# Norm, routing and token lists behind an output projection: block norms on VectorE, one routing chain for four blocks, ranks summed on TensorE, lists from rounded products

## What is computed

```python
x = layer_norm(DN_ALPHA * x + m, ln1_g[i], ln1_b[i])     # m: mixer output times w_o
f = hier_moe(x, ...)
x = layer_norm(DN_ALPHA * x + f, ln2_g[i], ln2_b[i])

def hier_moe(x, w_rg, b_rg, w_re, b_re, w1, w3, w2):
    g_prob = softmax(xt @ w_rg + b_rg)                   # 4 groups
    grp = argmax(g_prob); g_w = g_prob[grp]
    e_logits = (xt @ w_re + b_re).reshape(N, 4, 8)[grp]  # the 8 experts of that group
    top_v, top_i = lax.top_k(e_logits, 2)
    gate = softmax(top_v) * g_w
    expert = grp * 8 + top_i
    # every expert gets the list of its tokens; for each list:
    hdn = silu(xb @ w1[e]) * (xb @ w3[e])
    out[tokens] += (hdn @ w2[e]) * w
```

## Time and profile before

| | us |
|---|---|
| median of 3 runs | 3568.32 |
| fastest, slowest | 3567.33, 3570.15 |
| the profiled execution, its time | 3554.19 |
| its span | 3552.9 |

### The profile page before, as it was taken

How to read it: one execution, slowest core, us unless ns; L and a number is a source line. 1 busy time by engine, 2 the same in 40 slices (tenths; PEclk the granted TensorE clock), 3 DMA queues, 4 the chain that set the end, 5 groups by cost and what they waited for, 6 DMA issues and landing times. The chain is left out here.

```text
span 3552.9 us, 42265 instructions
## 1 busy us (share of the span) xinstructions
PE 3270.6 (92%) x16668; PEld 2719.4 (77%) x16669; DVE 2241.1 (63%) x3508; ACT 1801.9 (51%) x2689; POOL 394.9 (11%) x331
## 2 busy tenths in 40 slices
PE   8989899999989999999987999999789879999995
PEld 6789777877878777878766777788667868888874
DVE  5755343435855443333675888899743668988886
ACT  3333342323333342333462778888633628888884
POOL 1101000000101000000141111111100121111110
PEclk9988999999989999999998999999989989999998
DMA  4210122221120122222203899988722238898994
GB/s 139 72 56 1 64 79 95 95 81 63 50 80 1 48 95 75 93 88 89 72 1 110 327 351 364 359 348 353 301 71 103 80 144 336 357 361 356 361 359 178
DMA packets 135163, 590.99 MB, mean 166 GB/s; under 512 B 29616, under 2 KB 35632, under 8 KB 110256
## 3 DMA queue, kind: packets, MB, share of 16 engines
q1 hardware_dynamic: 115664, 569.92, 41.5%
q0 software_dynamic: 19296, 18.30, 2.2%
HBM read 594.40 MB, written 44.04 MB: 180 GB/s over the span
## 5 line engine op out<-in xcount | busy, mean ns | idle before, releaser
L189 PE MATMUL ps<-r,r 128*128 128x512 f32 (+4 forms) x11048 | 2593.7, 393 | 66.8 <-DVE r L2075 23.1
L189 PEld LDWEIGHTS ps<-r,r 128*128 128x128 f32 x11048 | 2046.2, 190 | 536.8 <-issue 63.8
L3463 DVE TENSOR_TENSOR r<-mem,r 128x1024 fp32r<-128x1024 f32 x768 | 902.5, 1220 | 133.6 <-ACT r L3408 127.3
L3408 ACT ACTIVATE r<-mem 128x1024 fp32r<-128x1024 f32 x768 | 788.3, 1061 | 226.5 <-PE ps L189 144.4
L692 ACT ACTIVATE r<-mem 128x512 fp32r<-128x512 f32 (+3 forms) x518 | 338.7, 661 | 906.4 <-PE ps L189 900.0
L727 DVE TENSOR_TENSOR r<-mem,r 128x512 fp32r<-128x512 f32 (+1 forms) x272 | 185.5, 688 | 436.6 <-ACT r L692 435.5
L729 DVE SCALAR_TENSOR_TENSOR r<-mem,r 128x512 fp32r<-128x512 f32 (+3 forms) x246 | 171.7, 714 | 263.6 <-ACT r L692 261.9
L3321 POOL DMA_INDIRECT xa<-mem,memu x64 | 101.5, 1587 | 964.7 <-ACT mem L3433 964.7
L3261 POOL DMA_INDIRECT mem<-xd,memu x64 | 99.2, 1550 | 84.2 <-PE ps L3343 35.1
L1666 PE MATMUL ps<-mem 128*128 128x65 f32 x800 | 99.8, 282 | 0.0
L1666 PEld LDWEIGHTS ps<-mem 128*128 128x128 f32 x800 | 96.7, 199 | 0.0
(11 more groups left out here) (392 smaller groups left out, 2883.2 us busy)
## 6 DMA issues: line engine op xcount, KB each, us to landing
mem<-in_w_up SPq DMA_DIRECT2D x80, 2048.0 KB, 18.5
mem<-in_w_down SPq DMA_DIRECT2D x80, 2048.0 KB, 7.9
mem<-in_w_gate SPq DMA_DIRECT2D x64, 2048.0 KB, 13.2
mem<-in_w_in SPq DMA_DIRECT2D x10, 2048.0 KB, 7.9
mem<-in_odd_w_qkv SPq DMA_DIRECT2D x6, 2048.0 KB, 8.4
mem<-in_w_o SPq DMA_DIRECT2D x4, 2048.0 KB, 10.4
mem<-in_rel SPq DMA_DIRECT2D x16, 512.0 KB, 3.3
mem<-in_even_w_in SPq DMA_DIRECT2D x3, 2048.0 KB, 8.0
```

The source lines that it names most:

```text
L189: r = e.matmul(out, a, b, start=start and i == 0, stop=stop and i == n - 1, skip_group_check=skip)
L3408: act.e.activation(wh, w, ACT.Copy).then_inc(*self.S["ex_wh"](self.l, e, i))
L3463: dve.e.tensor_tensor(wl, w, wh.bitcast(F32), SUB).then_inc(*self.S["ex_wl"](self.l, e, i))
```

## The change

All blocks' norms are on VectorE now, block t's between block t's moments and block t+1's sum; ScalarE's and GpSimd's parts are gone. The logits of blocks 0 and 1 are corrected among the blocks. TensorE computes the logits three matmuls later, and the logits of block 2 ahead of the turning of block 3. The group is found by a maximum and an equality, with the first among equals kept by a minimum; the masks of four blocks are made and added in one instruction each. TensorE adds the totals of earlier blocks onto the ranks by three more products in the same PSUM bank, so VectorE reads finished ranks. The comparison that makes `OS` is two instructions of 512, with rounded output. `OV` is rounded too: GpSimd writes the token number less 1024 (exact), the rounded gate, and what the rounding left out, 96 columns instead of 64. An empty place gives 0, and 0 + 1024 is a row beyond the end.

```diff
 # pe_blocks
-                if i == n - 3:
-                    if j >= 1:
-                        self.pe_turn(pe, j - 1)
-                    if j >= 2:
-                        self.pe_logits(pe, j - 2)
+                if i == n - 3 and j >= 1:
+                    self.pe_turn(pe, j - 1)
+                if i == n - 2 and j >= 2:
+                    self.pe_logits(pe, j - 2)
+        self.pe_logits(pe, 2)
         self.pe_turn(pe, 3)
-        self.pe_logits(pe, 2)
         self.pe_logits(pe, 3)
 # pe
-        pe.e.matmul(K.bank[0][:, 0:128], self.ustr, self.ohs, start=True, stop=True)
-        pe.e.matmul(K.bank[0][:, 128:256], self.ones, self.ohs, start=True, stop=True).then_inc(*S["rt_p"](l, "rank"))
-        pe.wait_ge("rt_v", l, "os")
-        mm(pe.e, K.bank[1][:, 0:64], [(self.OS[:, k, t, :], self.OV[:, k, t, :]) for k in range(2) for t in range(4)]).then_inc(
-            *S["rt_p"](l, "lists"))
+        pe.e.matmul(bank[:, 0:128], self.ustr, ohs, start=True, stop=False, skip_group_check=True)
+        for t in range(3):
+            o = bank[:, 32 * t + 32:128].rearrange("p (t n) -> p t n", n=32)
+            r = pe.e.matmul(o, self.ones, bc(ohs[:, 32 * t:32 * t + 32], 1, 3 - t), start=False, stop=t == 2,
+                            skip_group_check=True)
+        r.then_inc(*S["rt_p"](l, "rank"))
...
+        pe.wait_ge("rt_g", l, "values")
+        for k in range(2):
+            pe.wait_ge("rt_v", l, "os", k)
+            for t in range(4):
+                r = pe.e.matmul(K.bank[1][:, 0:96], self.OS[:, k, t, :], self.OV[:, k, t, :], start=k == 0 and t == 0,
+                                stop=k == 1 and t == 3)
+        r.then_inc(*S["rt_p"](l, "lists"))
 # dve_blocks
+        def norm(t):
+            x = K.X[:, t, :]
+            dve.wait_ge("d_ln", self.gains.names)
+            dve.wait_ge("rt_p", self.l, "turn", t, 1)
+            dve.then("ln_g", v.scalar_tensor_tensor(x, x, self.nmu[:, t:t + 1], self.gains.gb, ADD, MUL), sid, t)
+            v.scalar_tensor_tensor(x, x, self.mv[:, t, 1:2], self.gains.bb, MUL, ADD).then_inc(*S["ln_b"](sid, t))
         for t in range(4):
+            if t:
+                norm(t - 1)
+            if t == 3:
+                self.logits(dve, 0)
...
             job.dves(dve, self, job, t, self.acc(job, t)[:, 0:job.n])
             moments(t)
...
             roots(t)
+        self.logits(dve, 1)
+        norm(3)
 # route
+        dve.then("rt_v", v.tensor_reduce(self.gm, groups, AX.X, MAX))
+        v.tensor_tensor(goh, groups, bc(self.gm, 2, 4), ALU.is_equal).then_inc(*S["rt_v"](l, "goh"))
+        v.tensor_tensor(ge, groups, bc(self.gm, 2, 4), SUB).then_inc(*S["rt_v"](l, "ge"))
+        dve.wait_ge("rt_v", l, "goh")
+        dve.then("rt_v", v.tensor_tensor(goh, goh, bc(self.first, 1, 4), MUL))
+        dve.then("rt_v", v.tensor_reduce(self.mn, goh, AX.X, MIN))
+        dve.then("rt_v", v.tensor_tensor(goh, goh, bc(self.mn, 2, 4), ALU.is_equal))
+        dve.then("rt_v", v.tensor_scalar(goh, goh, 1.0, 1e30, SUB, MUL))
+        dve.then("rt_v", v.tensor_tensor(ml.rearrange("p t (g n) -> p t g n", g=4),
+                                         lg[:, :, 4:36].rearrange("p t (g n) -> p t g n", g=4), bc(goh, 3, 8), ADD))
...
+        dve.then("rt_v", v.tensor_tensor(oh, bc(bc(ei, 1, 4), 1, 2), bc(which, 3, 32), ALU.is_equal), l, "oh")
 # lists
+        dve.wait_ge("rt_p", l, "rank")
+        ranks = bank[0][:, 0:128].rearrange("p (t n) -> p t n", t=4)
+        dve.then("rt_v", v.tensor_tensor(self.ranked, self.oh, bc(ranks, 1, 2), MUL))
+        dve.then("rt_v", v.tensor_reduce(self.rv.rearrange("p t k -> p k t"), self.ranked, AX.X, ADD))
+        for k in range(2):
+            v.tensor_tensor(self.OS[:, k], bc(self.iota, 1, 4), bc(self.rv[:, :, k], 2, 128),
+                            ALU.is_equal).then_inc(*S["rt_v"](l, "os", k))
...
+        dve.then("rt_v", v.tensor_scalar(self.ixf, bank[1][:, 0:32], NONE, None, ADD))
+        v.tensor_copy(self.IDX[:, 1, :], self.ixf).then_inc(*S["rt_v"](l, "rows"))
+        dve.then("rt_v", v.tensor_copy(self.GT, bank[1][:, 32:64]))
+        v.tensor_tensor(self.GT, self.GT, bank[1][:, 64:96], ADD).then_inc(*S["rt_v"](l, "weights"))
 # pool
-            pool.wait_ge("ln_a", sid, t)
-            pool.then("ln_g", pool.e.tensor_tensor(x, x, self.gains.gb, MUL), sid, t)
-            pool.then("ln_b", pool.e.tensor_tensor(x, x, self.gains.bb, ADD), sid, t)
+        pool.wait_ge("rt_v", l, "oh")
+        p.tensor_tensor(OV[:, :, :, 0:32], self.oh, bc(self.val.rearrange("p t k -> p k t"), 3, 32), MUL)
+        pool.wait_ge("rt_v", l, "gt")
+        pool.then("rt_g", p.tensor_tensor(self.gates, self.oh, bc(self.gt.rearrange("p t k -> p k t"), 3, 32), MUL))
+        pool.then("rt_g", p.tensor_copy(OV[:, :, :, 32:64], self.gates))
+        p.tensor_tensor(OV[:, :, :, 64:96], self.gates, OV[:, :, :, 32:64].bitcast(F32), SUB).then_inc(*S["rt_g"](l, "values"))
```

141 lines of the change are left out of this document (43 added, 98 removed).

## The result

| | before | changed |
|---|---|---|
| median of the first comparison, us | 3567.82 (4 runs) | 3538.23 (4 runs, 3535.69 to 3547.28) |
| all runs of this study | 3567.2 (52 runs, 3550.2 to 3578.7) | 3541.2 (16 runs, 3524.8 to 3553.7) |
| the profiled execution, its span | 3554.19, 3552.9 | 3547.28, 3546.0 |

The ratio of the first comparison is 0.9932, 95% interval 0.9914 to 0.995. Two repeats, on two chips, gave 0.991 (0.9891 to 0.993) and 0.9938 (0.9919 to 0.9957).

A forecast was written before the change was run, and what follows sets the result against it. A serial chain, nearly all on VectorE, from the last block's sum to the first expert gather was taken as the bound. Gains 4.4 + 2.7 + 1.1 + 1.6 + 0.45 = 10.3 per layer: 3568.3 - 20.5 = 3547.8 us, range 3541 to 3556.

The forecast's parts named there:

- stall ahead of block 1's transposes: TensorE, ready to turn block 1, waits for block 0's norm and block 1's sum on VectorE: some 0.75 us.
- Step A: Norm of all blocks on VectorE, up to the route's start: 4.4 us gained per layer, give or take 1.
- step C: Ranks, gates and list operands, from `ohs` to the first list product: 5.25 us instead of 6.38, 1.1 gained per layer.
- rival (1): TensorE drops to half clock among the blocks: 3575.7 us, chance 0.03 in full; only after block 3, costs 1 to 2.
- Step B: The route for all blocks, up to `ohs`: 3.55 us instead of 6.24, 2.7 gained per layer.
- Step D: TensorE's list products: eight rounded matmuls in 2.1 us instead of sixteen passes in 3.67, 1.6 gained per layer (0.2 to 2.0).
- Step E: From the lists to the first gather: two small steps go, 0.45 us gained per layer.
- The difference between the profiled execution and the median: The median was 14.1 us longer than the profiled execution before; the forecast took this difference as unchanged.
- (2): VectorE and GpSimd collide more, GpSimd's operations taking twice the rows' size: 2.7 us more per layer, 3553.1 us, chance 0.08.
- (3): L3177's long steps were no waits for GpSimd, small two-input steps stay at 2.2 in places: 3557.3 us, chance 0.04.
- (4): Expert weights hold the start up, so an earlier gather is followed by a longer wait: 3566.3 us, chance 0.05.

The follow-up runs named there:

- no_pool_norm: The kernel before with GpSimd's six norm operations left out (no gain and bias for blocks 1 to 3): 3559.07 us in one run.
- norm_undone: The changed kernel with the norm as before and the logit corrections of blocks 0 and 1 behind the blocks again: 3550.95 us, ratio 0.9969.
- after_third: The changed kernel itself, measured a third time beside the kernel before: 3546.05 us (6 runs), ratio 0.9938.
- values_dve: The changed kernel with GpSimd's four operations for the list operands moved to VectorE: 3543.46 us (7 runs), ratio 0.9932.
- after_again: The changed kernel itself, measured again on another chip beside the kernel before: 3535.85 us (6 runs), ratio 0.991.

## Why the prediction was right

The forecast was 3547.8 us with 20.5 gained. The first comparison gave 3538.23, below the 3541 at which the range began; all sixteen runs of the changed kernel have the median 3541.2, just inside it, and the ratio times the 3568.3 that the forecast started from is 3544.0 (3537.6 to 3550.5). The sign and the chain were right, the changed stretch was within 1.5 us of it, and the range was too narrow below. By steps, layer 0, forecast and profile:

| step | forecast | first profile | three profiles, both layers |
|---|---|---|---|
| stall ahead of block 1's transposes | 0.75 | 0.63 | 0.61 to 0.63 |
| blocks' sums later by | 0.8 | 0.83 | 0.83 to 0.84 |
| block 3's sum to the route's first step | 6.4 | 6.32 | 6.32 to 7.58 |
| route, to `ohs` | 3.55 | 3.52 | 3.52 to 3.53 |
| `ohs` to the first list product | 5.25 | 4.26 | 4.26 |
| list products | 2.1 | 1.94 | 1.94 |
| lists to the gather | 1.32 | 1.31 | 1.31, in layer 1 1.56 |
| block 3's sum to the gather | 18.6 | 17.35 | 17.35 to 18.86 |

The sum fits better than its terms do. Step A came out smaller than forecast in five of the six places and step C larger in all six, and the two errors, of 0.7 and 1.0 us per layer, are of opposite sign: that part of the agreement is luck.

**Step A** holds in its mechanism, and in layer 0 of the first profile in its size: 11.60 became 6.32, less 0.83 in the blocks, 4.45 gained against 4.4. That place is the best of six. Its cause is the one named, by `no_pool_norm` and `norm_undone`. The Trainium skill's rule (SBUF — State Buffer, Who interferes with whom), that a VectorE instruction with two SBUF inputs and a GpSimd instruction that reads SBUF exclude each other for a whole instruction, stands behind the rows of these two kernels: 0.26 without GpSimd's work, 2.16 and 2.00 beside its 2.34 and 2.36, 0.17 for a reduction with one input at the same moment. One term varies that the forecast had only under a rival. The last 16 logit passes took 2.06 in the first profile, and in `after_third`

```profile
1949.60 3.17 PE L190 MATMUL ps<-mem 128*128 128x36 f32 x16 [0.80 <-ACT mem L3075]
```

since the clock fell a little earlier; `ohs` then comes 10.7 instead of 9.85 after block 3's sum. In the changed kernel's three profiles, both layers, block 3's sum to the route's first step is 6.32, 6.78, 7.21, 7.22, 7.16 and 7.58. So step A is worth 3.2 to 4.45 there, 3.7 on average. It is the mild form of rival (1), put at 1 to 2 us, and nearly always there.

**Step B** holds: 6.24 became 3.52. In `norm_undone` the same route steps gain only 1.1 from block 3's sum to `ohs`, as two of the new steps wait for GpSimd: part of B was to be had only with A.

**Step C** is the term that was mis-sized: 2.1 gained, not 1.1. The mechanism was right, as the comparisons alone take 1.29 and here 2.02. The mistake is in the sentence "they go one after another whichever is first", with both comparisons counted ahead of `values`. The rows show that the engines alternate: one comparison, the subtraction, the other comparison. Only one stands ahead of `values`, and the second runs while TensorE does the first four products, which need the first half of `OS` alone. Of the 1.38 charged for two comparisons the subtraction waits out 0.43 (1.05 less 0.62, what a product of its size takes), 0.95 less. GpSimd's own durations, 0.62, 0.40 and 0.62 where 0.73, 0.5 and 0.73 were taken from rows of other shapes, are 0.3 less, and the gates, which end 1.92 after `ohs` and not 1.7, take 0.2 of that back. The rule that GpSimd's part should rather be on VectorE, which the forecast weighed at nothing (GPSIMD Engine Reference, Engine selection, of the Trainium skill), was tried as `values_dve`: 0.24 us per layer slower in the rows. Here the rule would have cost a little.

**Step D** holds: 1.94 against 2.1, and 3.73 in fp32. **Step E** holds in layer 0: 1.31 against 1.32. In layer 1 it is 1.56 in all three profiles, 0.2 gained instead of 0.45; the cause is open. The gather's transfer took 5.00 where it had taken 4.87, and expert 0's weights (four subtractions, 4.63 from 1959.46) ended before its rows wanted them: TensorE's first product waits 0.74 behind VectorE's rounding of the rows, as before.

**The difference between the profiled execution and the median** is the other term that failed. The prediction said of these 14.1 us, "I know of no reason for that difference to move". They moved: the changed kernel's profiled execution is 9.05 longer than its median. The table of thirteen profiles shows where. The profiled execution of before was a quick one, with a rest of 3456.8, where thirteen profiles have 3466.6 on average; the first of the changed kernel had 3471.8. Whether that is chance alone is not shown: in all three comparisons of the changed kernel the profiled execution is the slowest or the second slowest. With the average rest, before comes to 3564.0 and the changed kernel (stretch 76.4, the mean of three) to 3543.0; the medians of 52 and 16 runs are 3567.2 and 3541.2. So 21 of the 26.0 us between those medians are the changed stretch. By a resampling of the runs the difference of means is 20.9 to 29.2, so the last 4 to 5 may be chance or a small effect behind the stretch. No run here settles it; `after_third`, with 21.1 between the medians, speaks for chance, `after_again`, with 28.0, does not.

The granted clock is the windows' answer to rival (1), the blocks first, then the steps behind them:

```profile
1927.00:1942.00 15.00, 14.37 (x94) 12.47 (x92) 13.63 (x26) 3.53 (x9) 0.00 (x0) 1.00 0.65 264
1942.04:1948.36 6.32, 4.63 (x39) 4.25 (x38) 5.80 (x15) 2.57 (x4) 0.00 (x0) 0.91 0.43 174
1948.36:1951.88 3.52, 0.00 (x0) 0.00 (x0) 3.18 (x22) 0.21 (x1) 0.00 (x0) 0.50 0.72 285
```

**The rivals.** (1) *Half clock among the blocks*: no; the stall came, 0.63, and the transposes behind it took 1.09, and the granted clock from 1927 to 1942 is 1.00. Only the logits behind block 3 pay, 0.5 to 1.3 in five of the six places. (2) *The engines collide more*: no; GpSimd's three took 0.62, 0.40 and 1.05 instead of twice the rows' size. (3) *The change does not do what it says*: no, by `no_pool_norm`. (4) *Expert weights hold the start up*: no; from the first transpose to the last expert it is 563.7 in layer 0 and 565.2 in layer 1, before 566.1 and 564.7, so an earlier gather was not paid back; the repeats have 564 to 567.
